# Decoder step, fp32 by three products: squares of the residual stream summed by another engine, and another order of work around each sublayer's end

## The reference, cut to what matters

```python
def rms_norm(x, g):
    return x * rsqrt(mean(x * x, axis=-1, keepdims=True) + EPS) * g

# every sublayer:  x = x + rms_norm(f(rms_norm(x, pre)), post)
x = x + rms_norm(sgu_mixer(rms_norm(x, pre_mix[0])), post_mix[0])     # update 1 stands behind this f
x = x + rms_norm(conv_ffn(rms_norm(x, pre_ffn[0])), post_ffn[0])      # update 2
kv = rms_norm(x, kv_in_g) @ w_dkv                                     # shared latent
x = x + rms_norm(mla_mixer(rms_norm(x, pre_mix[1])), post_mix[1])     # update 3
x = x + rms_norm(conv_ffn(rms_norm(x, pre_ffn[1])), post_ffn[1])      # update 4
# conv_ffn: a = h @ w_up; causal depthwise conv of width 3 over a; (gelu(g) * u) @ w_down
```

## Time and profile before

| | before |
|---|---|
| median of 3 runs | 1463.28 us |
| span of the profiled execution | 1461.2 us |
| PE busy | 1409.3 us (96%) |
| DVE busy | 894.1 us (61%) |
| ACT busy | 536.8 us (37%) |
| POOL busy | 175.0 us (12%) |
| granted TensorE clock, mean | 0.985 |

### The profile page before, as it was taken

How to read it: one execution, slowest core, us unless ns; L and a number is a source line. 1 busy time by engine, 2 the same in 40 slices (tenths; PEclk the granted TensorE clock), 3 DMA queues, 4 the chain that set the end, 5 groups by cost and what they waited for, 6 DMA issues and landing times.

```text
span 1461.2 us, 30495 instructions
## 1 busy us (share of the span) xinstructions
PE 1409.3 (96%) x11815; PEld 1329.9 (91%) x11815; DVE 894.1 (61%) x1518; ACT 536.8 (37%) x870; POOL 175.0 (12%) x329
## 2 busy tenths in 40 slices
PE   6999999998999999999999989998999999999997
PEld 5999999998999999999989855657999999999997
DVE  4444664227888888633375686464578888884334
ACT  4545443236222223333464212344543222223334
POOL 1000000000222222100001020100012322321000
PEclk9999999999999999999999999799999999999999
DMA  7332222321332232233425463101223233222331
GB/s 232 103 86 73 73 75 82 91 87 48 97 100 87 86 100 80 78 96 89 119 69 187 176 248 125 48 1 34 83 60 100 86 94 92 86 77 88 92 90 65
DMA packets 224370, 138.20 MB, mean 95 GB/s; under 512 B 12620, under 2 KB 220674, under 8 KB 223256
## 3 DMA queue, kind: packets, MB, share of 16 engines
q1 hardware_dynamic: 219688, 112.38, 26.5%
q0 software_dynamic: 4224, 24.62, 4.5%
q10 hardware_dynamic: 384, 0.16, 0.1%
HBM read 133.83 MB, written 3.67 MB: 94 GB/s over the span
## 4 chain that ended last, share of the span: by engine, by line
PE 91%; DVE 5%; ACT 2%; issue 1%; DMA 1%; SPq 0%; DVEq 0%; ACTq 0%
PE psum L659 76%; PE psum L1054 2%; PE psum L1183 1%; PE psum L1160 1%; PE psum L1037 1%; PE psum L718 1%; PE psum L1015 1%; PE psum L818 1%; PE psum L1163 1%; DVE ut L1686 1%; DVE x L1689 1%; DVE kt L1978 1%; DMA xn<-in_x_prompt 1%; PE psum L1172 1%; DVE wl L1647 1%
## 5 line engine op out<-in xcount | busy, mean ns | idle before, releaser
L1647 DVE TENSOR_TENSOR wl<-ws,wh 128x1024 fp32r<-128x1024 f32 x217 | 265.8, 1225 | 336.5 <-ACT wh L1243 173.5
L659 PE MATMUL psum<-xh,wh 128*128 128x260 f32 x2064 | 426.6, 285 | 11.0 <-DVE xl L1666 6.2
L659 PE MATMUL psum<-xh,wl 128*128 128x260 f32 x2064 | 421.5, 283 | 0.0
L659 PE MATMUL psum<-xl,wh 128*128 128x260 f32 x2064 | 420.6, 283 | 0.0
L659 PEld LDWEIGHTS psum<-xh,wh 128*128 128x128 f32 x2064 | 320.9, 189 | 14.3 <-issue 13.5
L659 PEld LDWEIGHTS psum<-xh,wl 128*128 128x128 f32 x2064 | 320.6, 189 | 0.0
L659 PEld LDWEIGHTS psum<-xl,wh 128*128 128x128 f32 x2064 | 320.0, 188 | 0.4
L1243 ACT ACTIVATE wh<-ws 128x1024 fp32r<-128x1024 f32 x144 | 152.2, 1057 | 319.1 <-PE psum L659 319.1
L659 PE MATMUL psum<-acth,wh 128*128 128x260 f32 x704 | 144.3, 284 | 0.0
L659 PE MATMUL psum<-acth,wl 128*128 128x260 f32 x704 | 143.2, 282 | 0.0
L659 PE MATMUL psum<-actl,wh 128*128 128x260 f32 x704 | 143.0, 282 | 0.0
(11 more groups left out here) (283 smaller groups left out, 1812.9 us busy)
## 6 DMA issues: line engine op xcount, KB each, us to landing
ws<-in_w_up SPq DMA_DIRECT2D x88, 512.0 KB, 3.8
ws<-in_w_in_a SPq DMA_DIRECT2D x32, 512.0 KB, 4.1
ws<-in_w_down SPq DMA_DIRECT2D x32, 384.0 KB, 3.4
ws<-in_w_down SPq DMA_DIRECT2D x32, 320.0 KB, 3.1
ws<-in_w_out_a SPq DMA_DIRECT2D x16, 512.0 KB, 3.9
ws<-in_w_o SPq DMA_DIRECT2D x8, 512.0 KB, 4.6
xn<-in_x_prompt SPq DMA_DIRECT2D x4, 512.0 KB, 10.1
ws<-in_w_dq SPq DMA_DIRECT2D x4, 512.0 KB, 4.6
```

Source lines behind the costliest of these rows:

```text
L659: mm = pe.matmul(psum[:, 2 * slot + b, 0:HB], w, r[:, k, b * HB:(b + 1) * HB], start=st, stop=en)
L1647: dve.tensor_tensor(low_, ws[:, slot4, :], f32(high), ALU.subtract).then_inc(w_low, 1)
```

## The change

On the squares: ACT squares the pairs into three places (`sq[:, 0]`, `sq[:, 1]`, `sqa`); POOL adds the four pairs of a half together, with three adds of [128 x 520] per half and six per update; PE then multiplies the sum of four pairs with the ones matrix once per half (`sum_half`, 2 matmuls), instead of four times (`sum_pair`). The sum of the first half stands behind the product of tile 3 of the second half, that of the second half inside the third unit, behind its first tile. `half_rms(name, 1)` moves from the end of `last_unit` behind the products of tile 1. On ACT the work of the last output tile's second half is moved between the first two `xh`, the rms of that half stands behind the squares of pair 1, that of `x` half 0 behind those of pair 6, the split of the third unit behind those of pair 4. On DVE, `low_half` is interleaved between `m * r2` and the add, with the first `xl` made two instructions earlier, and the split of the third unit goes from between the halves to the very end. In the MLP, DVE evacuates the first two tiles and splits the fourth unit before it convolves either. Update 4 keeps its order.

The diff, cut to its core:

```diff
+        def pair_squares(i):
+            return sqa[:, :] if i in (2, 4) else sq[:, 0, :] if i in (0, 6) else sq[:, 1, :]
 ...
+            def sum_squares(p):                                   # on POOL, ahead of mlp(0), behind it, ahead of mlp(1)
+                base, pooled = SQB[f"x{p}"], 6 * (p - 1)
+                for h in range(2):
+                    into = pair_squares(4 * h)
+                    for g in range(1, 4):
+                        pool.wait_ge(sq_done, base + 4 * h + g + 1)
+                        if g > 1:
+                            pool.wait_ge(sq_pooled, pooled + 3 * h + g - 1)
+                        pool.tensor_tensor(into, into, pair_squares(4 * h + g), ALU.add).then_inc(sq_pooled, 1)
 ...
                 mm.then_inc(mm_done, 1)
-                half_rms(name, 1)
+                if name == "m_ffn1":
+                    half_rms(name, 1)
 ...
-            def sum_pair(name, h, g):
-                i = 4 * h + g
-                if i == 0:
-                    pe.wait_ge(ln_done, SSB[name])
-                pe.wait_ge(sq_done, SQB[name] + i + 1)
+            def sum_half(p, h):
+                name = f"x{p}"
+                pe.wait_ge(ln_done, SSB[name])
+                pe.wait_ge(sq_pooled, 6 * (p - 1) + 3 * (h + 1))
                 for e in range(2):
-                    mm = pe.matmul(psum[:, 6 + h, 0:HB], ones[:, :], sq[:, i % 2, HALF[e]], start=(g == 0 and e == 0), stop=(g == 3 and e == 1))
-                mm.then_inc(ss_done if g == 3 else sq_summed, 1)
+                    mm = pe.matmul(psum[:, 6 + h, 0:HB], ones[:, :], pair_squares(4 * h)[:, HALF[e]], start=(e == 0), stop=(e == 1))
+                mm.then_inc(ss_done, 1)
 ...
-                        if t % 2:
-                            sum_pair(x_name, h, t // 2)
+                        if h == 0 and t == 1:
+                            half_rms(m_name, 1)
+                        if h == 1 and t == 3:
+                            sum_half(p, 0)
 ...
-                for u in range(2, 4):
-                    up(0, u, 2 if u == 2 else 1)
+                up(0, 2, 2, {1: lambda: sum_half(p, 1)})
+                up(0, 3, 1)
 ...
-            unit(U_KV + 2, weight_slot(U_KV + 2), 2, range(KD), xkh, xkl, True, True)
+            unit(U_KV + 2, weight_slot(U_KV + 2), 2, range(KD), xkh, xkl, True, True, between={1: lambda: sum_half(2, 1)})
 ...
+                def squares(i):                                   # on ACT
+                    h, g = i // 4, i % 4
+                    pooled = 6 * (p - 1)
+                    if 1 <= i < 3:
+                        act.wait_ge(ss_done, SSB[f"x{p}"])
+                    elif i == 6:
+                        act.wait_ge(ss_done, SSB[f"x{p}"] + 1)
+                    elif i >= 3:
+                        act.wait_ge(sq_pooled, pooled + {3: 1, 4: 2, 5: 3, 7: 4}[i])
+                    act.activation(halves(pair_squares(i)), x[:, 2 * g:2 * g + 2, HALF[h]], ACT.Square).then_inc(sq_done, 1)
+                high(0, 0)
+                last_square(1)
+                high(0, 1)
+                last_raw(1)
+                squares(0)
+                for i in range(1, 2 * KD // 2):
+                    for t in (2 * (i % 4), 2 * (i % 4) + 1):
+                        high(i // 4, t)
+                    squares(i)
+                    if i == 1:
+                        rms(name, r2, 1)
+                    elif i == 4:
+                        ahead_static(LOCKED[p])
+                    elif i == 6:
+                        rms(f"x{p}", r1, 0)
                 rms(f"x{p}", r1, 1)
 ...
+                for t in range(2):                                # on DVE
+                    scaled(0, t, 1)
+                    added(0, t, 1)
+                for i in range(1, KD):
+                    h, t = i // 4, 2 * (i % 4)
+                    hb, tb = (i - 1) // 4, 2 * ((i - 1) % 4)
+                    low_first = i == 1
+                    if low_first:
+                        low_half(p, tb, hb)
+                    scaled(h, t, 2)
+                    low_half(p, tb + (1 if low_first else 0), hb)
+                    added(h, t, 2)
+                    if not low_first:
+                        low_half(p, tb + 1, hb)
+                for t in (KD - 2, KD - 1):
+                    low_half(p, t, 1)
+                dve.wait_ge(x_new, base + 2 * KD)
+                ahead_static(LOCKED[p])
 ...
-                for u in range(4):
-                    tile(0, u, first=(u == 0), second=(u == 2))
+                for u in range(2):
+                    evacuate(0, u, first=(u == 0))
+                ahead(U_UP[l], 4, 0, 1)
+                for u in range(2):
+                    convolve(0, u)
+                for u in range(2, 4):
+                    tile(0, u, third=(u == 2))
```

More of the change, by code:

```diff
@@ L1283, in update, with last_square @@
                 sq_slot_free(name, KD - 1)
-                for h in range(2):
+                def last_square(h):
                     if h:
@@ L1442, in high_product, with tile @@
                     act.activation(acth[:, bass.ds(j, 1), :].rearrange("p o t -> p (o t)"), pr[:, :], ACT.Copy).then_inc(acth_ready, 1)
-                def tile(i, u, first=False):
-                    if not first:
-                        ahead(U_UP[l], 4, i, u)
+                def tile(i, u, first=False, second=False):
+                    if not second:
+                        ahead(U_UP[l], 4, i, 1 if first else u)
                     q, j = 4 * i + u, 2 * i + u // 2
@@ L1454, in mlp @@
                 for u in range(4):
-                    tile(0, u, first=(u == 0))
+                    tile(0, u, first=(u == 0), second=(u == 1))
                 with act.Fori(1, NF // 4) as i:
@@ new lines, in added @@
+                def added(h, t, n):
+                    dve.wait_ge(u_mul, base + KD * h + t + n)
+                    dve.tensor_tensor(x[:, t:t + n, HALF[h]], x[:, t:t + n, HALF[h]], place(h, t, n), ALU.add).then_inc(x_new, n)
+                if p == 4:
+                    for h in range(2):
+                        for t, n in ((0, 1), (1, 1), (2, 2), (4, 2), (6, 2)) if h == 0 else ((0, 2), (2, 2), (4, 2), (6, 2)):
+                            scaled(h, t, n)
+                            added(h, t, n)
+                    return
@@ L1830, in low_product, with evacuate @@
                                       f32(acth[:, bass.ds(j, 1), :]).rearrange("p o t -> p (o t)"), ALU.subtract).then_inc(actl_ready, 1)
-                def tile(i, u, first=False, second=False):
-                    q, j = 4 * i + u, 2 * i + u // 2
-                    f = (u % 2) * KF + j
-                    Q, J, b = NF * l + q, KF * l + j, u % 2
+                def evacuate(i, u, first=False, third=False):
+                    q = 4 * i + u
+                    Q, b = NF * l + q, u % 2
                     dve.wait_ge(mm_done, U_UP[l] + q + 1)
@@ L1856, in tile, with convolve @@
                                       ALU.mult).then_inc(evac_up, 1)
-                    if not first:
-                        ahead(U_UP[l], 4, i, u)
-                    if b == 0 and not first:
-                        low_product(j - 1)
+                def convolve(i, u):
+                    q, j = 4 * i + u, 2 * i + u // 2
+                    f = (u % 2) * KF + j
+                    Q, J, b = NF * l + q, KF * l + j, u % 2
                     dve.wait_ge(evac_up, Q + 1)
@@ L1881, in tile @@
                         dve.tensor_tensor(pr[:, SEQ:T], smp[0], smp[1], ALU.mult).then_inc(prod_done, 1)
-                for u in range(4):
-                    tile(0, u, first=(u == 0), second=(u == 2))
+                def tile(i, u, third=False):
+                    evacuate(i, u, third=third)
+                    ahead(U_UP[l], 4, i, u)
+                    if u % 2 == 0:
+                        low_product(2 * i + u // 2 - 1)
+                    convolve(i, u)
+                for u in range(2):
[5 more added lines that the diff above has]
+                    tile(0, u, third=(u == 2))
                 with dve.Fori(1, NF // 4) as i:
```

84 lines of the change are left out of this document (31 added, 53 removed).

## The result

| | before | after |
|---|---|---|
| median of 11 runs each, same chip (us) | 1464.83 (1462.51 to 1466.61) | 1467.47 (1465.06 to 1470.59) |
| ratio after to before | | 1.0024, 95% interval 1.0013 to 1.0034 |
| profiled execution: time, span (us), clock | its span and clock are in the table ahead | 1465.06, 1463.2, 0.989 |

The account below looks back on a forecast made before the run. PE was taken as the bound (2.30 us a pair), DVE next at 2.22; 8.9 us gained less 4.25 per update for POOL's adds gave 3.9 longer, 1467.2 us on the 1463.28 median; range 1453.5 to 1472.5.

Parts of the forecast that it names:

- DVE's order, PE's start: In the updates, DVE's interleaved low takes 2.03 us per pair of tiles; PE's first product comes 1.42 us earlier.
- The two waits on ACT: In an update, DVE waits for ACT's xh at tile 4 (0.67 us) and at tile 6 of the second half (1.9).
- The way without holds: From DVE's second small add to the MLP's fifth unit (update 2: query product), POOL's cost left out; update 3: 32.2 us.
- The 8.9 us: Gain over updates 1 to 3 without any cost of POOL's adds: 2.8 + 1.8 + 4.3 us.
- The split "with nothing to hide it": DVE's split of the third unit, now at the update's end, is uncovered: 1.23 us, then 0.14 until PE starts.
- The order in the MLP: PE's 1.5 us wait before the fourth unit goes; in update 1 the fifth starts at 366.4, 2.8 us gained.
- Update 2: Up to the query product: 1.8 us gained less 4.25 for POOL's adds, so 2.5 us lost.
- Update 3: 4.3 us gained, most because PE ran at a lower clock before, less 4.25 for POOL's adds: nothing.
- The hold: In updates, a begun POOL add delays DVE's next instruction with two SBUF inputs, about 1.15 us; 4.25 per update; chance 0.43.
- The sum: Whole kernel: update 1 loses 1.4 us, the second 2.5, the third nothing; 3.9 us longer.
- The clock: Rival: PE gets the lower clock for a whole update, costing 3 to 4 us each, about 1465; chance 0.04.
- not held: Rival: in the updates POOL's adds do not delay DVE, the 8.9 us gain stays, 1454.4 us; chance 0.30.

Follow-up runs that it names:

- write-only kernel: The changed kernel with each POOL add replaced by a fill of 1500 columns of unused memory that reads nothing; 1451.1 us, ratio 0.9919 to before.

## Why the prediction was right, step by step

- **DVE's order, PE's start:** right to the hundredth. First product 0.97 behind the anchor against 2.39, so 1.42 earlier; a block 2.02 (345.80 to 347.82) for 2.03.
- **The two waits on ACT:** 0.55 and 1.83 for 0.67 and 1.9.
- **The way without holds:** forecast 32.2, 27.25 and 32.2 from the anchors, measured in the write-only kernel 31.80, 27.06 and 31.77. The 8.9 us were 9.9, of which 2.6 are the lower clock that before had in updates 2 and 3. Most of it is the orders, as the kernel with the orders alone shows, and little of it the sums taken from PE, which the prediction did not price apart.
- **The split "with nothing to hide it":** wrong as a step, though its number (third unit 19.3 behind the anchor, measured 19.21 without holds) came out. PE's products of the last two tiles start with the last `low` and run 1.43 while the split runs 1.22. I had laid only DVE's line to its end and not PE's beside it, and the two end within 0.1 us of each other, so that the number came out is luck; moving the split gained 0.26 and not 1.1.
- **The order in the MLP:** right. No wait at the fourth unit; the fifth was at 35.81 with holds, 31.80 without.
- **Update 2:** 2.06 lost for 2.5. **Update 3:** 0.7 gained for 0; what was right in it is that before's low clock made this update look best.
- **The hold:** right in kind and place: adds 1 to 4 hold, 5 is free, 6 waits for the split (its record lasts 2.21, over the 1.9 that was named as the upper sign) and delays the sum by 0.50 (forecast 0.3). The price was 1.04 for 1.15, and 0.42 for 0.5 at the first. Per update 4.0 (35.81 less 31.80) for 4.25: the holds are 3.54 (third unit 22.72 less 19.21 is 3.51), the delay of the last sum 0.50. The estimate behind it was not right in its terms: an add lasts 1.29, not 1.15, but its last 0.25 doesn't hold. On the page of the Trainium skill, "SBUF — State Buffer", section "Who interferes with whom": the page has a VectorE instruction with two SBUF inputs contend with a GpSimd instruction that reads SBUF and not with one that only writes, and the runs agree: the add holds 1.04, the copy with one input 0.36, the memset nothing. They also agree that whichever comes first keeps the other waiting, but not quite for its whole length: the hold ends 0.20 to 0.25 short of it. The estimate of 1.14 by "GPSIMD Engine Reference", section 3.1, was under the measured 1.29.
- **The sum:** 3 x 4.0 less 9.9 is 2.2 longer, forecast 3.9; on the medians 2.6. The gain was forecast 1.0 too small and the cost 0.7 too large.
- **The clock:** update 1 of after had 0.93 in its window of 23 us, updates 2 and 3 had 1.00, and the third unit came 22.72, 22.70 and 22.71 behind the anchor, so it cost nothing there. That rival had assumed a whole update at the lower level; it didn't come.
- **The range:** the case "not held" was given 0.30, at 1454.4, 13 us below what came. The row that spoke for it (a split that lost only 0.05 beside a copy of 0.21) said little about a long add: a hold that is 0.20 to 0.25 shorter than the POOL instruction leaves next to nothing of a copy of 0.21, and the adds of 8 columns, 0.20 long, held no `low`.

## What to carry to other kernels

Work given to an idle engine isn't free if that engine reads the same memory as the one that sets the pace: here each POOL add of 1.29 us took 1.04 us from DVE, which would have made the add itself in 0.61. Before moving work, ask what the freed engine waits for next: PE's sums were worth 0.8 us once the orders were right, since DVE's pace and its two waits for ACT stood right behind. And test the parts of a change one by one: the kernel before with the two orders alone is 0.7% faster than before (some of it clock), with no sum moved.

## What the runs showed of the hardware

- The hold of a `low` is the POOL instruction's length less 0.25 us (1.29, 0.74 and 0.62 us), for one input or two, and that of an add of 520 columns its length less 0.20 (0.74 and 0.62); a MEMSET of 1.35 us beside DVE holds nothing. ACT isn't held: its squares that meet the adds of 339.11 and 341.25 last 0.62, for 0.64 before.

```profile
340.55 0.62 ACT L1343 ACTIVATE sqa<-x 128x520 f32<-128x520 f32 x1
...
342.64 0.62 ACT L1343 ACTIVATE sq<-x 128x520 f32<-128x520 f32 x1
```

- A POOL add that is ready while DVE works back to back is served at DVE's next change of instruction: it waited 0.07 to 0.49 us in four of six cases, and 0.92 behind the split of 1.22.
- DVE's multiplication and add in direct succession, the second waiting for the first's signal and reading its result, start 0.80 apart; with a `low` between them each costs 0.61 and 0.40. That is 0.19 us a pair which no table of waits shows.
